# Dense products of a hybrid decoder layer in one form, their results turned from staged rows; late value rows gathered by their own slots' waits

## The reference

```python
a = rms_norm(h, mix_norm)
proj = a @ w_in                       # 2048 x 4104: pool 1024, q, k, v of 8 heads x 128, 8 forget gates
y_pool = pool_mixer(...)              # trailing means over 2, 4, 8, 16 tokens minus the row, times pool_w
y_fox = forgetting_attention(...)     # causal, with summed log gates
h = h + concat(y_pool, y_fox) @ w_out
h = h + memory_cross_attention(rms_norm(h), rms_norm(mem), wq, wk, wv, wo)   # 4 heads of 512, all 2048 x 2048
h = h + peer_ffn(rms_norm(h), ...)
return rms_norm(h, final_norm)
```

## Time and profile before

| | us |
|---|---|
| three runs | 2039.21, 2043.6, 2041.2; median 2041.2 |
| profiled execution: its time | 2039.45 |
| its span | 2037.5 |
| TensorE busy | 1788.4 (88%) |
| VectorE busy | 1368.4 (67%) |
| GpSimd busy | 1022.5 (50%) |
| ScalarE busy | 560.0 (27%) |
| granted TensorE clock, mean | 0.947 |

### The profile page before, as it was taken

The page is one execution under the profiler, slowest core; times in us unless marked ns, Lnnn a source line. Parts: engine busy times, 40 slices in busy tenths (PEclk is TensorE's granted clock), DMA queues, the critical chain, the costliest instruction groups (busy, mean ns, idle before and its releaser), DMA issues.

```text
span 2037.5 us, 21513 instructions
## 1 busy us (share of the span) xinstructions
PE 1788.4 (88%) x7530; PEld 1188.6 (58%) x7531; DVE 1368.4 (67%) x2205; ACT 560.0 (27%) x1011; POOL 1022.5 (50%) x643
## 2 busy tenths in 40 slices
PE   7999999999999999765565578888877989999997
PEld 7998899888998898622222233444433544444442
DVE  4473453223324348899999988887888877888866
ACT  5334453345433520201010033223314620000001
POOL 4443343444332414566655554564555656777742
PEclk9999999999999999877777899999998999999998
DMA  8875454655546689999999999999999989999997
GB/s 208 239 174 147 141 184 155 197 190 186 167 145 198 194 287 399 344 421 418 417 418 415 410 402 398 402 416 402 404 417 401 397 302 403 385 410 378 397 421 318
DMA packets 157650, 647.41 MB, mean 318 GB/s; under 512 B 25894, under 2 KB 31086, under 8 KB 95598
## 3 DMA queue, kind: packets, MB, share of 16 engines
q0 software_dynamic: 73728, 450.98, 54.7%
q1 hardware_dynamic: 83824, 195.16, 29.5%
HBM read 729.91 MB, written 2.10 MB: 359 GB/s over the span
## 4 chain that ended last, share of the span: by engine, by line
PE 61%; DMA 18%; DVE 14%; issue 4%; POOL 2%; ACT 0%; DVEq 0%; POOLq 0%; SPq 0%; ACTq 0%
PE acc L1813 8%; PE misc L1813 8%; DMA u_ring<-in_peer_u_dram,idx 7%; DMA v_high<-in_peer_v_dram,idx 7%; PE acc L1469 5%; PE acc L1471 5%; PE acc L1470 5%; PE acc L1476 5%; PE acc L1477 5%; PE acc L1478 5%; DVE product L1314 5%; DVE product L1316 5%; PE misc L1778 4%; PE acc L1758 3%; DMA v_low<-in_peer_v_dram,idx 1%
## 5 line engine op out<-in xcount | busy, mean ns | idle before, releaser
L486 POOL TENSOR_TENSOR w_lo<-raw,w_hi 128x1024 fp32r<-128x1024 f32 x112 | 273.4, 2441 | 430.0 <-ACT w_hi L583 429.6
L1778 PE MATMUL misc<-v_high,diag 128*128 128x512 f32 x512 | 268.1, 673 | 104.9 <-DMA v_high<-in_peer_v_dram,idx 96.9
L1778 PE MATMUL misc<-v_low,diag 128*128 128x512 f32 x512 | 274.0, 688 | 93.5 <-DMA v_low<-in_peer_v_dram,idx 77.6
L583 ACT ACTIVATE w_hi<-raw 128x1024 fp32r<-128x1024 f32 x224 | 237.0, 1060 | 352.7 <-PE acc L1478 171.5
L910 DVE TENSOR_TENSOR w_lo<-raw,w_hi 128x1024 fp32r<-128x1024 f32 x112 | 149.3, 1334 | 266.1 <-ACT w_hi L583 266.0
L526 POOL DMA_INDIRECT u_ring<-in_peer_u_dram,idx x160 | 210.0, 1313 | 192.7 <-DVE dots L1316 136.5
L1469 PE MATMUL acc<-t_hi,w_hi 128*128 128x256 f32 x896 | 255.9, 286 | 0.0
L1470 PE MATMUL acc<-t_lo,w_hi 128*128 128x256 f32 x896 | 253.9, 283 | 0.0
L1471 PE MATMUL acc<-t_hi,w_lo 128*128 128x256 f32 x896 | 253.9, 283 | 0.0
L1778 PEld LDWEIGHTS misc<-v_low,diag 128*128 128x128 f32 x512 | 108.0, 220 | 249.7 <-issue 137.9
L1778 PEld LDWEIGHTS misc<-v_high,diag 128*128 128x128 f32 x512 | 105.2, 215 | 253.1 <-DMA v_high<-in_peer_v_dram,idx 133.0
(11 more groups left out here) (262 smaller groups left out, 2665.2 us busy)
## 6 DMA issues: line engine op xcount, KB each, us to landing
u_ring<-in_peer_v_dram SPq DMA_DIRECT2D x48, 1024.0 KB, 8.9
raw<-in_w_in_dram SPq DMA_DIRECT2D x64, 512.0 KB, 5.2
raw<-in_xattn_wk_dram SPq DMA_DIRECT2D x32, 512.0 KB, 4.8
raw<-in_xattn_wv_dram SPq DMA_DIRECT2D x32, 512.0 KB, 3.7
raw<-in_w_out_dram SPq DMA_DIRECT2D x32, 512.0 KB, 4.7
...
```

The lines of the kernel that those rows point to most:

```text
L486: nc.gpsimd.tensor_tensor(w_lo[:, j % RING, :, :], raw[:, j % RING, :, :], w_hi[:, j % RING, :, :].bitcast(F32), ALU.subtract).then_inc(lo ...
L1778: ins = nc.tensor.matmul(o, diag[:, n % 4, :], v_slot(n % VS)[:, i * CW:(i + 1) * CW], start=False, stop=False)
```

## The change

Part 1. `products` loses its `turned` form: all items have stationary activations and 512 moving weight columns. The fourteen items that were turned are evacuated into staging tiles (`rows_a`, `rows_b`, `rows_k`, `rows_q`, two slots each) by `evacuate`; beside the next item, after its second chunk, TensorE turns them with eight 128x128 transposes into two `misc` banks (`turn_rows`), and ScalarE copies each bank to where the channels were (`rows_out`, two 128x512 copies), between the splits of chunks 5 and 6 (`beside_rows`). Readers wait for `rows_copied`. The turn of the last in item that is turned stands after the first chunk of the first v item of in. Turns of the last two k items stand in the first v item (after chunks 3 and 5), because the item between is full of `fox_values`; the last q item is turned after `x_turn(0)`, and `x_turn(1)` now stands before `x_scores(3)`. x_scores(i) moves from after the fourth to after the fifth chunk. The window sums move: the output tile `diff` lies on `rows_a`, so window_diff(3) waits until row 3 is turned and stands behind the split of chunk 5; (2) and (1) follow the evacuation of item 4, (0) that of item 5. Some hardware loops are unrolled.

Part 2. Late slots are taken in the order 4, 6, 0, 1, 5, 2, 3, and slots 4, 5, 6 each wait for their own last reader instead of for all dot products. The last two takes of block 0 (126, 127) move behind dense tiles 0 and 1. The scatters of the last two periods end at k = 12 instead of k = 15. LATE is 116: TensorE sums four late rows (117 to 123) ahead of the shared last three instead of six.

```diff
+    rows_a = put("rows_a", [P, 2, TT, CW], F32, at_t2 + 16 * KB)
+    rows_b = put("rows_b", [P, 2, TT, CW], F32, at_f)
+    rows_k = put("rows_k", [P, 2, TT, CW], F32, at_v + 8 * KB)
+    rows_q = put("rows_q", [P, 2, TT, CW], F32, at_v + 16 * KB)
...
+        def staged(r):
+
+            if r < ROW_K:
+                return (rows_a if r < 4 else rows_b)[:, r % 2]
+            return (rows_k if r < ROW_Q else rows_q)[:, r % 2]
+
+        def channels(r):
+
+            if r < ROW_K:
+                return foxT[:, r * CT:(r + 1) * CT]
+            return memk[:, (r - ROW_K) * CT:(r - ROW_K + 1) * CT] if r < ROW_Q else qs[:, r % 2]
+
+        def row_bank(r, half):
+
+            if r < ROW_Q:
+                return 2 * (r % 2) + half
+            return (0 if r == ROW_Q + 1 else 2) + half
...
+        LAST_K = 11
...
-            return range(b + (k - 2) * 8 // 14, b + (k - 1) * 8 // 14)
+            return range(b + min((k - 2) * 8 // LAST_K, 8), b + min((k - 1) * 8 // LAST_K, 8))
 
         def u_turn(n):
 
             return sum(u_index(i) == u_index(n) for i in range(n + 1))
 
-        LATE = TILE0 - TOP
+        LATE = TILE0 - TOP + 4
 
         SHARED = TILE0 - 3
         BY_PE = (SHARED - 1 - LATE) // 2
@@ -375,7 +402,7 @@
 
         def late_slot(m):
 
-            return (m + 4) % V2S
+            return (4, 6, 0, 1, 5, 2, 3)[m % V2S]
 
         def high_bank(i):
 
@@ -568,7 +595,7 @@
                 elif slot < VS:
                     pool.wait_ge(v_used, TILE0 - VS + slot + 1)
                 else:
-                    pool.wait_ge(dot_done, GROUPS * TOP)
+                    pool.wait_ge(dot_done, (PH * TOP, GROUPS * TOP, last_dot(6) + 1)[slot - VS])
                 gather_v(TILE0 + m, slot, late_landed[slot])
 
 
+
+            def rows_out(r):
+                for half in range(2):
+                    act.wait_ge(rows_T, 2 * r + half + 1)
+                    nc.scalar.activation(channels(r)[:, 2 * half:2 * half + 2, :], misc[:, row_bank(r, half), :].rearrange("p (a s) -> p a s", a=2),
+                                         ACT.Copy).then_inc(rows_copied, 1)
+
+            def beside_rows(n, r):
+                high_parts(n, 1, chunks=(HALF, HALF + 1))
+                rows_out(r)
+                high_parts(n, 1, chunks=(HALF + 2, HALF + 3))
 
             act.wait_ge(zero_ready, 1)
...
             high_parts(1, 0)
-            with act.Fori(1, 3) as n:
-                high_parts(n, 1)
+            for n in (1, 2):
+                beside_rows(n, n - 1)
                 high_parts(n + 1, 0)
...
             fox_hi(FH - 1)
             n0, items = ITEMS["v"]
-            with act.Fori(0, items) as i:
+            high_parts(n0, 1, chunks=range(HALF, CH - 1))
+            rows_out(ROW_K + 2)
+            high_parts(n0, 1, chunks=(CH - 1,))
+            high_parts(n0 + 1, 0, chunks=(0,))
+            rows_out(ROW_K + 3)
+            high_parts(n0 + 1, 0, chunks=range(1, HALF))
+            with act.Fori(1, items) as i:
                 high_parts(i + n0, 1)
                 high_parts(i + (n0 + 1), 0)
...
             step(nc.vector.memset(winB[:, :, 0:pad], 0.0))
+            low_parts(4, 1, chunks=(HALF + 1,))
+            dve.wait_ge(rows_T, 2 * 4)
+            dve.wait_ge(rows_copied, 2 * 2)
             window_diff(3)
-            low_parts(4, 1, chunks=(HALF + 1,))
-            window_diff(2)
...
             low_parts(T_IN, 0, chunks=(1,))
-            evacuate_T(5, 1, foxT[:, 5 * CT:6 * CT, :])
+            evacuate(5, 1, staged(5))
             low_parts(T_IN, 0, chunks=(3,))
+            window_diff(0)
 
             def score_max(u):
...
                 if m == 3:
                     weights(GROUPS - 1)
-                if m == LATE:
+                if m == TILE0 - TOP:
                     first_sums()
-                if m == LATE + 3:
+                if m == TILE0 - TOP + 2:
                     gained(0)
-                if m == LATE + 5:
+                if m == TILE0 - TOP + 3:
                     scaled(0)
                 if m == SHARED:
...
                         kt = j * KC + kk
                         first, last = kt == 0, kt == KT - 1
-                        if turned:
-                            for ct in range(CT):
-                                o = acc[:, q, ct // 2, ct % 2 * S:(ct % 2 + 1) * S]
-                                wh, wl = (w[:, s, kk, ct * P:(ct + 1) * P] for w in (w_hi, w_lo))
-
-                                nc.tensor.matmul(o, wh, hi[:, kt, :], start=first and ct % 2 == 0, stop=False, skip_group_check=True)
-                                nc.tensor.matmul(o, wh, lo[:, kt, :], start=False, stop=False, skip_group_check=True)
-                                ins = nc.tensor.matmul(o, wl, hi[:, kt, :], start=False, stop=last and ct % 2 == 1, skip_group_check=True)
-                        else:
-                            for t in range(TT):
-                                o = acc[:, q, t, :]
-                                xh, xl = (a[:, kt, t * P:(t + 1) * P] for a in (hi, lo))
-                                nc.tensor.matmul(o, xh, w_hi[:, s, kk, :], start=first, stop=False)
-                                nc.tensor.matmul(o, xh, w_lo[:, s, kk, :], start=False, stop=False)
-                                ins = nc.tensor.matmul(o, xl, w_hi[:, s, kk, :], start=False, stop=last)
+                        for t in range(TT):
+                            o = acc[:, q, t, :]
+                            xh, xl = (a[:, kt, t * P:(t + 1) * P] for a in (hi, lo))
+                            nc.tensor.matmul(o, xh, w_hi[:, s, kk, :], start=first, stop=False)
+                            nc.tensor.matmul(o, xh, w_lo[:, s, kk, :], start=False, stop=False)
+                            ins = nc.tensor.matmul(o, xl, w_hi[:, s, kk, :], start=False, stop=last)
                     ins.then_inc(chunk_used, 1)
...
 
+            def turn_rows(r, item):
+
+                pe.wait_ge(acc_free, item + 3)
+                for half in range(2):
+                    for a in range(2):
+                        for t in range(TT):
+                            c = 2 * half + a
+                            ins = nc.tensor.transpose(misc[:, row_bank(r, half), a * S + t * P:a * S + (t + 1) * P],
+                                                      staged(r)[:, t, c * P:(c + 1) * P], ident[:, :])
+                    ins.then_inc(rows_T, 1)
+
+            def turn_in(r):
+                if r < 2:
+                    pe.wait_ge(tr_lo, PAIRS)
+                else:
+                    pe.wait_ge(rows_copied, 2 * (r - 2) + 2)
+                if r == 4:
+                    pe.wait_ge(fa_ready, 1)
+                turn_rows(r, r)
+
...
             for p in range(4):
                 normed_pair(p)
-            products(0, 0, t1_hi, t1_lo, True, ready=(tr_lo, 0),
+            products(0, 0, t1_hi, t1_lo, ready=(tr_lo, 0),
                      between={j: lambda j=j: [normed_pair(p, -3) for p in (4 + 2 * j, 5 + 2 * j)] for j in range(2)})
-            products(1, 1, t1_hi, t1_lo, True)
-            products(2, 0, t1_hi, t1_lo, True)
-            products(3, 1, t1_hi, t1_lo, True)
+            products(1, 1, t1_hi, t1_lo, between={1: lambda: turn_in(0)})
+            products(2, 0, t1_hi, t1_lo, between={1: lambda: turn_in(1)})
+            products(3, 1, t1_hi, t1_lo, between={1: lambda: turn_in(2)})
 
             pe.wait_ge(wf_ready, 1)
+            pe.wait_ge(rows_copied, 2 * 2 + 1)
             o = misc[:, 0, 0:S]
             for kt in range(KT):
                 nc.tensor.matmul(o, wf_hi[:, kt, :], t1_hi[:, kt, :], start=kt == 0, stop=False)
                 nc.tensor.matmul(o, wf_hi[:, kt, :], t1_lo[:, kt, :], start=False, stop=False)
                 ins = nc.tensor.matmul(o, wf_lo[:, kt, :], t1_hi[:, kt, :], start=False, stop=kt == KT - 1)
             ins.then_inc(f_done, 1)
-            products(4, 0, t1_hi, t1_lo, True)
-            products(5, 1, t1_hi, t1_lo, True)
+            products(4, 0, t1_hi, t1_lo, between={1: lambda: turn_in(3)})
+            products(5, 1, t1_hi, t1_lo, between={1: lambda: turn_in(4)})
 
             def fox_scores(u):
                 f, t = u // TT, u % TT
+                if u % CH == 0:
+                    pe.wait_ge(rows_copied, 2 * (5 + u // CH))
                 if u >= 2:
                     pe.wait_ge(qk_read, u - 1)
...
                 if g >= 2:
                     pe.wait_ge(pool_copied, g - 1)
+                else:
+                    pe.wait_ge(rows_copied, 2 * T_IN)
                 for dt in range(GT):
                     for ct in range(GT):
                         ins = nc.tensor.matmul(misc[:, pool_bank(g), dt * S:(dt + 1) * S], poolw[:, g, ct, dt * P:(dt + 1) * P],
@@ -1564,6 +1623,8 @@
                            None if free is None else tr_lo, free)
 
             def beside_values(item, j):
+                if item == 0 and j == 0:
+                    turn_in(T_IN - 1)
```

(31 more changed lines are left out.)

66 lines of the change are left out of this document (37 added, 29 removed).

## The result

The changed kernel takes 2045.7 us (median of 20 runs, 2042.55 to 2056.03) against 2041.3 us (20 runs, 2038.51 to 2044.79) before. The ratio is 1.0024, 95% interval [1.0016, 1.0032]: 5 us slower by the ratio and 4.4 by the medians, where 5 us faster was forecast. The time lies outside the forecast's range of 2030 to 2044.

The account below looks back on a forecast made before the run. It took TensorE to bound the dense stage and DMA the gather stage. Part 1 (-17.5 + 11.3 + 1.1 = -5.1 us) plus part 2 (0) took 2041.2 to 2036.1 us; range 2030 to 2044, the forecast's own 2033.5 to 2039.5.

Parts of the forecast that it names:

- The 14 x 1.25 us and the 13 x 0.87 us: Dense stage: fourteen items in the plain form save 17.5 us; thirteen turnings beside other items cost 11.3 us back.
- The turning at the end of q: Last q item, turned where TensorE already waits: first x_values 1.1 us later than 617.21.
- The edits taken at nothing: Dense stage: ScalarE's copies hidden, moved window sums priced 0 (up to 2.2 us possible), unrolled loops cost nothing.
- The two cancel: part 2 is 0: Hand-over and tail: DMA 2.3 us behind at the start, 2.3 us regained at the end; bounds -5.6 and +9.7.
- The new hole: Hand-over: late rows 5 and 6 wait for takes 126 and 127 behind dense tiles; DMA 2.3 us behind by 1680.
- The head start: Hand-over: TensorE ends dense tile 2 at 1678.2 instead of 1680.7, 2.5 us ahead.
- The give-back at the end: Tail: late rows 113 and 115 go to VectorE, GpSimd skips a 4.88 us wait; 2.3 us regained by bytes.
- the early rows: Hand-over: late rows 0 to 3, issued before the last dot products end, fill the old DMA hole.
- The value queue stands still: Hand-over rival, chance 0.12: early rows worthless, DMA idles behind late rows 5 and 6; part 2 +9.7, total +4.6, 2045.8 us.
- TensorE decides the tail: Tail rival, chance 0.28: TensorE's 2.5 us at the start and 3.1 us at the end count; -10.7 us, 2030.5 us.
- The dense gain is eaten: Dense-stage rival, chance 0.18: waits for turnings or late splits cost about 5 us over 14 items; 2041.2 us.
- the signs named for a wrong forecast: TensorE waiting for a split in item 4, 6 or 9; last gathers over 3 us off their distance from the last dot product.

Follow-up runs that it names:

- the dense part alone: Part 1 with late value rows, waits, takes, scatters and LATE as in the kernel before; 2038.7 us, ratio 0.9982 to the kernel before.
- With only the scatters bunched: Part 1 plus, of the hand-over, only the bunched scatters, against the kernel before; 2038.2 us, ratio 0.9985.
- With the takes ahead: The changed kernel with takes 126 and 127 back ahead of the dense tiles, all else as changed; 2035.7 us, ratio 0.9978 to the kernel before.
- three pairs, above: Pairs of kernels differing only in LATE, 116 against 112: ratios 0.9978 and 0.9967, 0.9968 and 0.9971, 0.9978 and 0.9985.
- the two comparisons that isolate it: Changed kernel with slots reordered so the queue is free: 0.39%, 8 us, under it. Takes ahead of tiles with gathers held: 0.33%, 6.7 us, over that without hold.
- the held queue (1.0011): Changed kernel with takes 126 and 127 ahead of the tiles, late gathers 5 and 6 made to wait for the first two tiles; 2044.7 us, ratio 1.0011.
- four variants: Takes back ahead of tiles in the changed kernel: otherwise as changed 0.9978, with LATE 112 0.9967, with scatters spread 0.9968, with both 0.9971.

## Why the prediction failed

**Part 1 was right.** Forecast -5.1 us; measured -4.4 us in the traces (the start of `x_values`) and -3.7 us in the times, with an interval from -1.8 to -5.5 that holds the forecast. The 14 x 1.25 us and the 13 x 0.87 us are in the items as 22.65 us; at the last evacuation of q 5.84 us of the forecast 6.2 were there. The turning at the end of q took 1.45 us instead of 1.1: ScalarE's copy ended 0.30 us after the second `x_turn`. The edits taken at nothing cost nothing: window_diff(3) ran from 121.78 to 128.6 and window_diff(0) from 161.44 to 166.1, and TensorE waited for neither.

**The step that failed is "The two cancel: part 2 is 0".** Measured, part 2 cost 7.4 us [4.5, 10.0]. Three of its terms were wrong, and so was the way in which it added them.

*The new hole.* The text has TensorE do "tile 0 by 1657.6, take 126 by 1661, ... take 127 by 1671.3". Measured: tile 0 at 1662.3, take 126 at 1665.7, take 127 at 1676.0, 4.7 us later throughout. An earlier sentence says why: "Tile 0's rows are requested after the same dot product as before and land 10.6 us later, 1647.6 to 1649." It is the same dot product, the fourth from the end, but it ended 7 us later. SyncE's requests of the first three tiles, in the changed kernel and then in the dense part alone:

```profile
1644.20 5.38 SPq L490 DMA_DIRECT2D u_ring<-in_peer_v_dram  x3
```
```profile
1635.43 8.59 SPq L490 DMA_DIRECT2D u_ring<-in_peer_v_dram  x3
```

Before they went out at 1637.04. In the changed kernel VectorE's last four dot products end in one burst, from 1644.1 to 1651.7, where those of the dense part alone end from 1635.3 to 1648.5. Ahead of the burst VectorE waits for a scatter on TensorE, to build the next one's operand, and the dot products behind it in its program wait too:

```profile
1640.74 0.55 DVE L1344 TENSOR_TENSOR hotB<-listsT,keys 96x384 f32<-96x384 f32 x1 [4.90 <-PE acc L1888]
```

With only the scatters bunched the request is at 1642.34, so it is the bunching that gathers them. (With the scatters spread again in the changed kernel it is at 1637.12, and tile 0 waits for the last scatter instead and starts at 1650.47: the hold is hardly shorter, and so is the time.) So late rows 5 and 6 went out at 1666.67 and 1676.97 instead of some 1661 and 1671. In the forecast's own stretch, 1630 to 1680, the DMA engines did 36.7 us of work where the sum has 37.6, 3.2 us behind the kernel before instead of 2.3; from 1630 to 1700 it is 4.2 us (14.0 idle against 9.8).

*The head start.* "TensorE is 2.5 us ahead": measured, tile 2 ended 32.4 us after the last dot product began, and 32.0 us in the kernel before. With the takes ahead, under the tile's own DMA wait, it ends after 26.3 us. The text knew that TensorE would come cold from a wait for tile 0's rows, with the scatters done by 1643 and the rows there at 1649, and didn't ask whether the takes would have fitted into that wait.

*The give-back at the end.* The end did run at a share of 1.01 from 1960 to 2030, but the time was no shorter for it. `LATE` 116 by itself gave nothing (three pairs, above), where the text has 2.3 us.

*The adding up.* The sum counts an idle microsecond of DMA before the last dot product and one behind it as the same, so that the early rows could pay for the new hole. Even with its terms measured it comes to 3.2 to 4.2 us, not 7.4. In the times the early rows are worth 2.0 to 2.6 us and the held queue costs 7 to 9. The comparison that was left out is with the same early rows and *no* hold: against the takes ahead of the tiles, the DMA engines idle 10.5 us more from 1630 to 1700 (14.0 against 3.5), GpSimd has issued six late rows fewer by 1690 (14 against 20), and the time is 9.4 us longer.

**The rivals.** *The value queue stands still* is what happened, with a chance of 0.12 and a price of 2045.8 us; measured 2045.7. Its place and sign were right; that its time is right to 0.1 us is luck. It added 9.7 us of part 2 to -5.1 us of part 1, and measured they are 7.4 and -3.7. The hold cost 7 to 9 us in the two comparisons that isolate it (forecast 8.2), the bunched scatters 0.9 us with 1.4 either way (forecast 1.5), and the early rows, which it takes as worth nothing, gave 2.0 to 2.6 us. The argument against it, that idle DMA engines before 1650 can do the early rows' work, is true in the main: the share there is 1.01 and 0.92 and was 0.73 and 0.70, though the engines were not idle all that time (the prediction's own stretch from 1640 to 1642 has a total share of 0.98, most of it in the queue that loads the tiles). It doesn't answer the rival, as this work is worth less than the hold costs. *TensorE decides the tail* is refuted by the kernel with only the bunched scatters, whose first tile starts 5.2 us sooner at the same time. *The dense gain is eaten* is refuted by the dense part alone. Of the signs named for a wrong forecast one appeared: the gathers end further from the last dot product. The last is issued 370.9 us behind it, 361.7 before, and the span ends 6.5 us further from it. A share under 0.7 for 20 us (0.46 and 0.50) was itself forecast, as a sign of the right mechanism; so was row 6 some 20 us behind row 4, and it came 24.4 us behind.

**What stays open.** How much of the 0.13% between the held queue (1.0011) and the changed kernel (1.0024) is TensorE's order: the lengths of the holds (14.85 us in sum against 20.88) could account for it, but no run separates them. Why holds of 5 us, as with the scatters spread, cost nothing that shows. And by what path a held queue costs its time.

**The best version** is the dense part with the late rows' own waits and both takes ahead of the tiles: 0.9967 to 0.9978 in four variants, 4.5 to 6.7 us under the kernel before by the ratios and some 10 us under the changed one. Between the four (scatters spread or bunched, `LATE` 112 or 116) these runs can't choose.
